# MoBA attention: the relative bias is added by VectorE from a skewed table, two heads' scores are issued before the last input tile, and a head pair's value products alternate

## What is computed

```
q = to_heads(q) * (Dh ** -0.5)                       # 8 heads of 64
bias_own = rel_bias[:, rel_bucket(q_pos[:, None] - own_pos[None, :])]
s_own = jnp.einsum('bhqd,bhkd->bhqk', q_c, k_own).astype(f32) + bias_own.astype(f32)[None]
s_own = jnp.where(own_pos[None, :] <= q_pos[:, None], s_own, -jnp.inf)
probs = jax.nn.softmax(logits, axis=-1).astype(v.dtype)
...
jnp.einsum('bhqk,bhkd->bhqd', p_own, v_own)
```

## Time and profile before

| | us |
|---|---|
| median of the 3 runs | 2477.56 |
| the runs | 2479.95, 2473.61, 2477.56 |
| span of the profiled execution | 2475.7 |
| TensorE busy | 2411.7 (97%) |
| VectorE busy | 1606.0 (65%) |
| ScalarE busy | 1033.3 (42%) |
| MoBA stage of layer 0, first bias matmul to first transpose of the solver | 302.98 to 327.75 |
| MoBA stage of layer 1, the same | 1001.31 to 1026.08 |

### The profile page before, as it was taken

The page is one execution under the profiler, slowest core; times in us unless marked ns, Lnnn a source line. Parts: engine busy times, 40 slices in busy tenths (PEclk is TensorE's granted clock), DMA queues, the critical chain, the costliest instruction groups (busy, mean ns, idle before and its releaser), DMA issues. The chain is left out here.

```text
span 2475.7 us, 41693 instructions
## 1 busy us (share of the span) xinstructions
PE 2411.7 (97%) x17447; PEld 2055.0 (83%) x17447; DVE 1606.0 (65%) x2242; ACT 1033.3 (42%) x1365; POOL 99.2 (4%) x179
## 2 busy tenths in 40 slices
PE   7999999999999999999999999999999999998999
PEld 7999989999999999899999854464888887647999
DVE  6887756778888887657798632671744442474555
ACT  5445534454554455335454321661422222263333
POOL 2010000001101100000001000000000000000000
PEclk9999999999999999999999999999999999999999
DMA  8776503647777775116467742102532331212452
GB/s 283 251 271 216 168 3 120 205 145 267 252 254 239 272 244 160 46 54 213 162 229 255 272 155 68 52 2 71 167 102 90 98 102 52 81 56 69 162 195 69
DMA packets 270807, 381.97 MB, mean 154 GB/s; under 512 B 9593, under 2 KB 235209, under 8 KB 268994
## 3 DMA queue, kind: packets, MB, share of 16 engines
q1 hardware_dynamic: 251628, 314.47, 38.7%
q0 software_dynamic: 18128, 64.20, 7.2%
q10 hardware_dynamic: 902, 1.15, 0.2%
HBM read 366.13 MB, written 13.65 MB: 153 GB/s over the span
## 5 line engine op out<-in xcount | busy, mean ns | idle before, releaser
L704 PE MATMUL ps<-span 128*128 128x512 f32 x1280 | 453.9, 399 | 2.3 <-issue 1.2
L635 PE MATMUL ps<-span,w_low 128*128 128x256 f32 x1440 | 408.0, 283 | 0.0
L706 PE MATMUL ps<-span,w_low 128*128 128x256 f32 x1280 | 359.5, 281 | 0.0
L633 PE MATMUL ps<-span 128*128 128x256 f32 x1216 | 348.6, 287 | 8.2 <-DVE span L1585 5.2
L1603 DVE TENSOR_TENSOR w_low<-ring,span 128x2048 fp32r<-128x2048 f32 x131 | 299.8, 2288 | 82.3 <-ACT span L1267 82.3
L1267 ACT ACTIVATE span<-ring 128x2048 fp32r<-128x2048 f32 x131 | 250.6, 1915 | 135.5 <-DMA ring<-in_ffn_w_in 112.8
L704 PEld LDWEIGHTS ps<-span 128*128 128x128 f32 x1280 | 240.6, 188 | 60.3 <-issue 1.3
L635 PEld LDWEIGHTS ps<-span,w_low 128*128 128x128 f32 x1440 | 277.0, 192 | 0.0
L634 PE MATMUL ps<-span 128*128 128x256 f32 x864 | 245.3, 284 | 0.0
L633 PEld LDWEIGHTS ps<-span 128*128 128x128 f32 x1216 | 233.8, 192 | 12.4 <-DVE w_low L1603 5.4
L706 PEld LDWEIGHTS ps<-span,w_low 128*128 128x128 f32 x1280 | 241.9, 189 | 0.0
(11 more groups left out here) (487 smaller groups left out, 5337.3 us busy)
## 6 DMA issues: line engine op xcount, KB each, us to landing
ring<-in_ffn_w_in SPq DMA_DIRECT2D x88, 1024.0 KB, 8.9
ring<-in_w_mlp SPq DMA_DIRECT2D x64, 1024.0 KB, 5.3
wmod<-in_w_mod POOLq DMA_DIRECT2D x96, 512.0 KB, 6.8
ring<-in_ffn_w_out SPq DMA_DIRECT2D x44, 1024.0 KB, 5.2
ring<-in_w_mix_in SPq DMA_DIRECT2D x26, 1024.0 KB, 5.5
ring<-in_xattn_w_kv SPq DMA_DIRECT2D x16, 1024.0 KB, 5.4
mod_scratch<-mod_acc POOLq DMA_DIRECT2D x24, 512.0 KB, 6.2
ring<-mod_scratch SPq DMA_DIRECT2D x12, 1024.0 KB, 4.9
```

The lines of the kernel that those rows point to most:

```text
L633: mm(dst, w_hi, x_hi, start=start, stop=False, **more)
L635: return mm(dst, w_lo, x_hi, start=False, stop=stop, **more)
L704: mm(ps[bank + m].rearrange("p (w t) -> p w t", w=2), hi[:, k, cols], span[:, :, k, :], start=(k == 0), stop=False, skip_group_check=True)
L706: last = mm(ps[bank + m][:, 0:T], lo[:, k, cols], h_high[:, k, :], start=False, stop=(k == KD - 1), skip_group_check=True)
```

## The change

VectorE adds the bias. The table `toep` takes the place of `hank`: partition p holds the bias row of a head shifted so that it lies as the scores need it. It is loaded from a DRAM scratch that holds each head's row 16 times, in eight DMAs of 16 partitions each. The two `flip` matmuls of each head and the constant `flip` are gone; `maxima` uses `tensor_tensor_reduce`, one instruction that adds the table to the bank, writes the sum back to the bank and leaves the maximum. The banks of heads are (2, 3, 0, 1, 4, 5, 0, 1). Heads 0 and 1 have their scores issued before the 13th tile, and their exponentials stand on ScalarE's list ahead of the copy of that tile. The value products of two heads are issued together, in turn.

```diff
+MOBA_BANKS = (2, 3, 0, 1, 4, 5, 0, 1)
+BIAS_ROWS = 16
+BIAS_READY = 16 + P // BIAS_ROWS * 16
...
             def scores(h):
-                pair, hb, bank = h // 2, (h % 2) * HD, ps[SCORE_BANKS[h % 4]]
-                if h >= 4:
+                pair, hb, bank = h // 2, (h % 2) * HD, ps[MOBA_BANKS[h]]
+                if h >= 6:
                     pe.wait_ge(*sm_act.at(l, 2 * (h - 3)))
                 hi = slice(hb, hb + HD)
-
-                mm(bank[:, 0:T], cst["flip"], hank[:, h, :], start=True, stop=False,
-                   skip_group_check=True)
-                mm(bank[:, T:T + P], cst["flip"], hank[:, h, P:T], start=False, stop=False,
-                   skip_group_check=True)
-                mm(bank[:, 0:T], mq[hi, pair, P:T], mk[hi, pair, :], start=False, stop=False,
-                   skip_group_check=True)
-                mm(bank[:, T:T + P], mq[hi, pair, 0:P], mk[hi, pair, 0:P], start=False, stop=True,
-                   skip_group_check=True).then_inc(*sc_done.up())
+                mm(bank[:, 0:T], mq[hi, pair, P:T], mk[hi, pair, :], start=True, stop=True)
+                mm(bank[:, T:T + P], mq[hi, pair, 0:P], mk[hi, pair, 0:P], start=True, stop=True
+                   ).then_inc(*sc_done.up())
...
-            def out(h):
...
-                mm(dst, mv[:, 0, cols], probT[:, e, 0:T], start=True, stop=False, skip_group_check=True)
-                last = mm(dst[:, P:T], mv[:, 1, cols], probT[:, e, T:T + P], start=False, stop=True,
-                          skip_group_check=True)
-                last.then_inc(*av_done.up())
+            def out_pair(pair):
+                pe.wait_ge(*pt_ready.at(l, 2 * pair + 2))
+                if pair >= 2:
                     pe.wait_ge(*av_out.at(l, pair - 1))
+                bank = ps[6 + pair % 2]
+                for k, at, width in ((0, 0, T), (1, P, P)):
+                    for e in range(2):
+                        h = 2 * pair + e
+                        last = mm(bank[e * HD:(e + 1) * HD, at:T], mv[:, k, h * HD:(h + 1) * HD],
+                                  probT[:, e, k * T:k * T + width], start=(k == 0), stop=(k == 1),
+                                  skip_group_check=True)
...
+            def attend(first, end):
+                if first == 0:
+                    pe.wait_ge(*mix_evac.at(l, 10))
+                    pe.wait_ge(*act_step.at(l, ACT_KK_STD))
+                else:
+                    pe.wait_ge(*dve_step.at(l, DVE_FEATURES))
+                    pe.wait_ge(*mix_evac.at(l, MIX_TILES - 1))
+                for h in range(first, end):
+                    step(h)
+
+            def step(h):
                 if h < NH:
                     scores(h)
+                if h >= 4 and h % 2 == 0:
+                    out_pair((h - 4) // 2)
                 if 2 <= h < NH + 2:
                     turn(h - 2)
-                if h >= 3:
-                    out(h - 3)
+                if h == NH + 1:
+                    out_pair(NPAIR - 1)
...
                     head_sums(tmp, 0)
-            pe.wait_ge(*dve_step.at(l, DVE_FEATURES))
-            moba(l)
+                    attend = moba(l)
+                    attend(0, 2)
+            attend(2, NH + 2)
...
-                pool.dma_start(hank[:, :, :], bass.AP(src.tensor, 0, [[1, P], [2 * T, NH], [1, T]])
-                               ).then_inc(bias_stored.sem, 16)
+                for p in range(0, P, BIAS_ROWS):
+                    pool.dma_start(toep[p:p + BIAS_ROWS, :, :], bass.AP(
+                        src.tensor, P - 1 - p, [[2 * T - 1, BIAS_ROWS], [BIAS_ROWS * 2 * T, NH], [1, T]])
+                        ).then_inc(bias_stored.sem, 16)
...
                 elif j >= 11:
+                    if n == MIX_TILES - 1:
+                        act.wait_ge(w_used[FIRST_AT[("mix_in", j)] % RING].sem, freed(FIRST_AT[("mix_in", j)], l) + 1)
+                        exponential, turned = softmax(l, 0, 1.0, (T, P), MOBA_BANKS)
+                        exponential(0)
+                        exponential(1)
                     take(l, ("mix_in", j), mix_bank(n), mv[:, :, (j - 11) * BLK:(j - 10) * BLK], mix_evac)
...
+                    if biases:
+                        v.tensor_tensor_reduce(bank[:, at:at + w], bank[:, at:at + w], biases(h, t), 1.0,
+                                               -3.0e38, ALU.add, ALU.max, smx[:, e, t:t + 1]).then_inc(*sm_max.up())
+                    else:
+                        v.tensor_reduce(smx[:, e, t:t + 1], bank[:, at:at + w], AX_X, ALU.max
+                                        ).then_inc(*sm_max.up())
...
+            if l == 0:
+                dve.wait_ge(bias_stored.sem, BIAS_READY)
+            maxima, weights = softmax(l, 0, 1.0, (T, P), MOBA_BANKS, lambda h, t: toep[:, h, t * P:T])
```

More of the change, by code:

```diff
@@ L270, in program @@
         store["v_loaded"] = [Signal(ctx, nc, f"v_loaded{s}") for s in range(RING2)]
-        scratch = {"bias": nc.dram_tensor("bias_scratch", (NH, 2 * T), F32).ap(),
+        scratch = {"bias": nc.dram_tensor("bias_scratch", (NH, BIAS_ROWS, 2 * T), F32).ap(),
                    "mod": nc.dram_tensor("mod_scratch", (DEPTH, P, 2, MODS * P), F32).ap()}
@@ L809, in turn @@
                 last.then_inc(*pt_done.up())
[L811 to L814 removed]
+            def out_pair(pair):
+                pe.wait_ge(*pt_ready.at(l, 2 * pair + 2))
+                if pair >= 2:
                     pe.wait_ge(*av_out.at(l, pair - 1))
[L816 to L825 removed]
+                bank = ps[6 + pair % 2]
[5 more added lines that the diff above has]
+                                  skip_group_check=True)
+                        if k == 1:
+                            last.then_inc(*av_done.up())
+            def attend(first, end):
[8 more added lines that the diff above has]
+            def step(h):
                 if h < NH:
                     scores(h)
+                if h >= 4 and h % 2 == 0:
+                    out_pair((h - 4) // 2)
                 if 2 <= h < NH + 2:
                     turn(h - 2)
[L830 to L831 removed]
+                if h == NH + 1:
+                    out_pair(NPAIR - 1)
+            return attend
         def heads_of(e):
@@ L1469, in scalar_program @@
             col_high(l, KV0)
-            exponential, turned = softmax(l, 0, 1.0, (T, P), SCORE_BANKS)
-            for h in range(NH + 2):
+            for h in range(2, NH + 2):
                 if h < NH:
@@ L1969, in vector_program @@
             step(l, v.memset(state[:, :, :], 0.0), seq_step)
-            maxima, weights = softmax(l, 0, 1.0, (T, P), SCORE_BANKS)
+            if l == 0:
+                dve.wait_ge(bias_stored.sem, BIAS_READY)
+            maxima, weights = softmax(l, 0, 1.0, (T, P), MOBA_BANKS, lambda h, t: toep[:, h, t * P:T])
             evac = moba_out(l)
```

24 lines of the change are left out of this document (7 added, 17 removed).

## The result

| | before | after |
|---|---|---|
| median, us (6 runs each) | 2476.64 | 2484.86 |
| least to most, us | 2473.17 to 2481.05 | 2482.86 to 2488.96 |
| span of the profiled execution, us | 2475.7 | 2480.6 |
| mean granted clock over it | 0.994 | 0.986 |

The ratio of the times is 1.0033, with a 95% interval of 1.0021 to 1.0044. The forecast was 2473.2 in a range of 2466 to 2480; the change is slower, by 4.9 us more than the range's upper end.

What follows compares the result with a forecast made beforehand. TensorE's list was taken to bound the MoBA stage; most of its shed ten microseconds would become waits, leaving 2.2 us a layer: 2475.7 - 4.4 + 1.9 = 2473.2 us, range 2466 to 2480.

Steps and rivals of the forecast that it cites:

- what the stage gains is passed on: Behind the MoBA stage, solver and memory tiles keep TensorE busy 90.20 of 92.25 us, so the stage's gain carries through.
- TensorE has spare time between: In the changed stage TensorE's work per head is 1.73 us, VectorE's 1.79 plus the 2.20 us piece.
- Price x of the fused instruction: VectorE's add and maximum for both parts of a head: 0.80 us; 0.1 us of it is 0.5 us a layer.
- Value products of a pair: TensorE's four products for two heads in turn take about 0.80 us, not 1.58; 3.1 us less a layer.
- The early scores: Scores of heads 0 and 1 ahead of the 13th tile take 2 x 0.85 = 1.70 us on TensorE.
- The hole of 2.3 us: TensorE stands 2.3 us ahead of head 2's scores, awaiting ScalarE's copy of the 13th tile; it stood 0.73 before.
- The stage's walk: Step-by-step sum through layer 0's MoBA stage: solver starts at 325.68 instead of 327.75; gain taken as 2.2 us a layer.
- The table costs nothing: The 256 KB bias table, loaded by GpSimd from 219.82, is there before 245; VectorE asks for it at 300.56.
- x = 1.21: Rival: VectorE's fused instruction runs at the running sums' rate or near; 2477.3 us, no change; chance 0.14.
- products that don't overlap: Rival: value products in turn do not overlap, 2.3 us a layer lost, no gain, 2477.8 us; chance 0.06.
- TensorE alone sets the end: Rival: TensorE's list alone ends the MoBA stage, gaining 8.1 us a layer, 2461.4 us; chance 0.07.
- x = 1.42: Rival: VectorE's fused instruction costs an add and a maximum pass; a layer loses 0.9 us, 2479.4 us; chance 0.08.

Runs made afterwards that it cites:

- bias_left_out: The kernel before without the two bias products of each head and nothing in their place; 2486.23 us, ratio 1.0035.
- pad_all: The changed kernel with dead products: 20 behind the 13th tile, 3 ahead of each turn, 8 ahead of each value pair; 2476.17 us, ratio 0.9999.
- take_first: The changed kernel with ScalarE's copy of the 13th tile ahead of the exponentials of heads 0 and 1; 2482.40 us, ratio 1.0030.
- pairs_only: The kernel before with only the value products of two heads issued in turn, bias still on TensorE; 2482.37 us, ratio 1.0019.
- early_only: The kernel before with only heads 0 and 1 moved ahead of the 13th tile, bias still on TensorE; one execution, 2483.11 us.
- pad_first: take_first with dead products: 5 behind the 13th tile, 3 ahead of each turn, 8 ahead of each value pair; 2476.53 us, ratio 0.9999.
- early_timed: The same kernel as early_only (heads 0 and 1 early, bias on TensorE), timed over 10 runs; 2483.69 us, ratio 1.0032.
- dead_bias: The changed kernel with two dead products of the old bias products' size ahead of each head's scores; 2495.27 us, ratio 1.0080.
- dead_filled: dead_bias with 20 more dead products in the hole ahead of head 2's scores; 2485.77 us, ratio 1.0023.
- thin_flips: The kernel before with bias products on 64 of the 128 rows, half of the bias left out; one execution, 2474.05 us.
- fill_hole: The changed kernel with 5 dead fp32 products between the 13th tile and head 2's scores; 2485.32 us, ratio 1.0025.
- pad_more: pad_first with more dead products: 8 behind the 13th tile, 5 ahead of each turn, 12 ahead of each value pair; 2478.75 us, ratio 1.0011.
- pad_late: no_early with dead products: 5 behind the 13th tile, 3 ahead of each turn, 8 ahead of each value pair; 2485.53 us, ratio 1.0030.
- table_only: The kernel before with only the bias moved to VectorE; order, banks and single value products as before; 2487.05 us, ratio 1.0044.
- no_early: The changed kernel with all eight heads' scores behind the 13th tile and exponentials behind its copy; 2484.10 us, ratio 1.0033.

## Why the prediction was wrong

**The step that failed** is in the first part: "what the stage gains is passed on", with, in the sum, "TensorE has spare time between" and "most of the ten microseconds that TensorE sheds turn into waits for VectorE and ScalarE". I priced these waits, and the 2.3 us of standing ahead of head 2, at their own length. I had read the granted clock of 1.00 in the stage and left it at 1.00 in every later step. It was no constant: with the waits it went to 0.50 in both layers of the changed kernel and of every part of the change that takes work from TensorE. No rival of mine had it, and all of my bounds were for the price of one instruction. bias_left_out, which only removes work and is 1.0035 slower, shows that this alone suffices, and pad_all, which only adds dead work and is back at 0.9999, that the clock accounts for the difference.

The Trainium skill (TensorE: Matmul & The Clock Gate, "What's actually happening") says that the throttled clock is the default and activity is what releases it. The windows of after agree for the fall, 1.00 and then 0.50 behind a hole of 2.39 us. For the return they don't: TensorE is busy 3.40 of 3.40 us from 307.20 on and stays at 0.50, and in layer 1 the full clock comes back while it waits. Nothing in them shows which measure of activity the chip takes.

**Point by point.**
- *Price x of the fused instruction*, taken 0.80, bounds 0.62 to 1.42: right, 0.74. The half rate of the Trainium skill (Vector Engine (DVE) Microarchitecture Reference, "Points that are easy to get wrong") names two sources in SBUF; here one is in PSUM, and the rate was not halved: 256 columns take 0.43, as a plain copy does (0.42).
- *Value products of a pair*, 0.80: right, 0.81 in take_first. But pairs_only, the edit by itself, does not gain: it makes a pause of 1.83 us and 6.8 us at half clock.
- *The early scores*, taken 2 x 0.85 = 1.70: wrong, 0.86 for both heads, since they ran side by side. The rows before had no two heads' scores next to each other.
- *The hole of 2.3 us*: right, 2.39. That the move "costs as much as it gains" isn't shown: early_only, at full clock and with no work shed, only loses, 1.6 and 1.7 a layer, and at full clock with the work shed the order with the hole (pad_all, stages 32.0, the hole filled with dead products) is 0.9 behind the one without (pad_first, 31.1). Wrong in its kind: a pause of that length is also where the clock falls.
- *The stage's walk*: near for a TensorE at full clock, in part by luck. pad_all has the value products of pairs 2 and 3 at 321.41 and 324.73 (forecast 321.72 and 324.16) and the solver at 326.31 (forecast 325.68). But two errors cancel in this. From the head sums to the scores of head 2 it takes 11.1 us where the forecast has 11.7, and from there to the solver 20.4 (305.90 to 326.31) where it has 19.4. The stage gains 1.6 us a layer where I had 2.2, and the solver behind it gives 0.7 and 0.1 back, which "what the stage gains is passed on" left out. So at full clock, dead products included, the two layers gain 2.5 us of the 4.4.
- *The table costs nothing*: right, neither layer shows a wait for it.
- *The rivals*: x = 1.21 and 1.42 and products that don't overlap all fell with the prices. "TensorE alone sets the end" came true in a way that I had not thought of: it set the end because it ran at half speed.
- *The range*: its upper end of 2480 came from x = 1.42. The measured 2484.9 needed a mechanism, not a larger x.

**What stays open.** Which measure of TensorE's activity decides. Pauses do not order the runs by themselves: the hole of 2.39 us was followed by a fall in five of the eight stages profiled with it unfilled (after, early_timed, early_only, dead_bias), pauses of 0.78 and 0.61 us by one in take_first's layer 1, and 1.99 us in dead_filled and 1.19 in thin_flips by none. Nor does busy time: in after TensorE is busy 3.40 of 3.40 us right behind the fall and stays at 0.50. Long pauses alone suffice where the bias products are in place (early_timed, pairs_only); whether thinner work alone suffices no run tells, since no run thins the work and keeps it free of pauses. I also can't say why dead_bias's unprofiled runs are up to 18 us slower than its profiled one.

## What to carry to other kernels

Before taking work from TensorE in a stage where another engine sets the pace, read the granted clock there and ask what thinner work and new pauses will do to it: here 6.6 us less work a layer cost 9 us in all (bias_left_out), since at half clock the engine with spare time becomes the bound. A wait of 2 us on TensorE is to be priced not only at 2 us but with a good chance of the next 7 to 30 us at half speed, and shorter waits are not safe (fill_hole). Dead products in the pauses are a cheap test of whether a slow stage is slow by its clock, and here gave the time back, but they don't turn a saving of TensorE's work into a gain by themselves.

## What the runs showed of the hardware that was not expected

- Longest pause of TensorE in a stage, and how long the clock stood at 0.50 from its fall in that stage on (profiled executions, layer 0 / layer 1). The fall does not always come behind that pause, see below the table:

| kernel | longest pause, us | at 0.50, us |
|---|---|---|
| before | 0.73 / 0.78 | none / none |
| pad_first, pad_all, pad_more | up to 0.71 | none |
| thin_flips | 1.19 / 1.19 | none / none |
| take_first | 1.64 / 1.64 | 17.1 / 23.9 |
| fill_hole | 1.64 / 1.64 | 23.9 / 23.9 |
| pairs_only | 1.83 / 1.83 | 6.8 / 6.8 |
| dead_filled | 1.99 / 1.99 | none / none |
| bias_left_out | 2.06 / 2.06 | 20.5 / 20.5 |
| pad_late | 2.26 / 2.22 | 6.8 / 6.8 |
| table_only | 2.26 / 2.23 | 23.9 / 23.9 |
| no_early | 2.26 / 2.22 | 30.7 / 23.9 |
| early_only; early_timed (same kernel) | 2.39 / 2.39 | none / none; 10.2 / 6.8 |
| dead_bias | 2.39 / 2.39 | 13.7 / none |
| after | 2.39 / 2.39 | 27.3 / 20.5 |

In take_first and fill_hole the fall comes ahead of the longest pause, in table_only and in no_early's layer 0 inside it. The same kernel falls or not from one execution to the next (early_only and early_timed), so one execution at full clock proves little.
- Products on different halves of the rows ran side by side when they came in turn: two records start at 303.83 in thin_flips, and a stage is 1.6 us shorter with the same number of instructions. The two early heads' scores of after do the same: 0.86 us for both, where one head's scores take 0.85 by themselves.
- VectorE's fused add and maximum from one PSUM and one SBUF source runs at the rate of a copy, 0.43 us for 256 columns, with 0.14 for each accumulator read.
